# The expert stage of a 13-stage network on one NeuronCore: token rows fetched by a slot table, no rows of zeros written at the start, expert weights in 2 MB transfers

## The reference

```python
h = rms_norm(x, norm_g) * (1 + scale) + shift                 # 512 x 1024
grp = argmax(softmax(h @ w_router_group))                     # 4 groups
e_logits = (h @ w_router_expert) of the 4 experts in grp
top_p, top_i = top_k(softmax(e_logits), 2)                    # 2 of 16 experts per token
weight = p_group[grp] * top_p / sum(top_p)
y[token] = sum over its 2 experts e of weight * (silu(h @ w1[e]) * (h @ w3[e])) @ w2[e]
x = x + gate * y
```

## Time and profile before

| | us |
|---|---|
| median of three runs | 3839.18 |
| profiled execution | 3840.37 |
| its span | 3838.6 |
| first instruction of the first feed-forward | 60.5 |
| first MoE, from its first instruction to the first instruction of hgrn | 2565.0 to 2967.8 |
| its expert loop, first weight matmul | 2645.3 |
| second MoE, from its first instruction | 3431.2 |
| its expert loop, first weight matmul | 3511.8 |

### The profile page before, as it was taken

One profiled execution on the slowest core, in us unless ns is written; L12 is line 12 of the kernel. 1 busy time (PEld: TensorE's weight loads), 2 busy tenths in 40 slices (PEclk: granted clock), 3 DMA queues, 4 the chain that ended last, 5 costly groups with the idle time before them and its releaser, 6 DMA issues. The chain is left out here.

```text
span 3838.6 us, 39125 instructions
## 1 busy us (share of the span) xinstructions
PE 3356.0 (87%) x15102; PEld 2590.3 (67%) x15102; DVE 2047.6 (53%) x2698; ACT 1328.2 (35%) x1710; POOL 220.4 (6%) x241
## 2 busy tenths in 40 slices
PE   2999998899989999888999797885995987685995
PEld 2888765788878887567888585464884454544884
DVE  2555415455445544255554544545886256735886
ACT  2322215222222222243222324623884121313884
POOL 0000000000000000000000003422001000012001
PEclk9999898999999999989999897987997999886998
DMA  8333231333223323304331411025995211025995
GB/s 273 139 148 113 89 109 33 126 148 135 84 110 148 148 88 113 111 1 159 148 131 55 153 33 67 1 103 220 413 414 214 94 44 44 23 80 212 416 415 216
DMA packets 89600, 553.78 MB, mean 144 GB/s; under 512 B 9376, under 2 KB 10272, under 8 KB 41200
## 3 DMA queue, kind: packets, MB, share of 16 engines
q1 hardware_dynamic: 71760, 485.76, 32.8%
q0 software_dynamic: 13088, 49.29, 3.6%
q10 hardware_dynamic: 4608, 16.78, 1.1%
HBM read 524.49 MB, written 48.28 MB: 149 GB/s over the span
## 5 line engine op out<-in xcount | busy, mean ns | idle before, releaser
L211 PE MATMUL ffn_gate_up<-ffn_h_high,ffn_gate_up_high 128*128 128x512 f32 x1408 | 548.3, 389 | 7.1 <-DVE ffn_h_low L245 7.1
L213 PE MATMUL ffn_gate_up<-ffn_h_high,ffn_gate_up_low 128*128 128x512 f32 x1408 | 548.0, 389 | 0.0
L212 PE MATMUL ffn_gate_up<-ffn_h_low,ffn_gate_up_high 128*128 128x512 f32 x1408 | 547.8, 389 | 0.0
L2244 DVE TENSOR_TENSOR moe_low<-moe_raw,moe_high 128x2048 fp32r<-128x2048 f32 x192 | 433.7, 2286 | 38.9 <-ACT moe_high L2151 38.6
L454 ACT ACTIVATE ffn_silu_gate<-ffn_gate_up 128x512 f32<-128x512 f32 x88 | 52.7, 598 | 970.2 <-PE ffn_gate_up L213 970.2
L2151 ACT ACTIVATE moe_high<-moe_raw 128x2048 fp32r<-128x2048 f32 x192 | 364.2, 1917 | 19.4 <-PE moe_bank L213 19.4
L485 DVE TENSOR_TENSOR ffn_product<-ffn_silu_gate,ffn_gate_up 128x512 f32<-128x512 f32 x88 | 60.5, 687 | 564.4 <-ACT ffn_silu_gate L454 564.4
L211 PEld LDWEIGHTS ffn_gate_up<-ffn_h_high,ffn_gate_up_high 128*128 128x128 f32 x1408 | 264.3, 188 | 63.2 <-DVE ffn_h_low L245 8.4
L213 PEld LDWEIGHTS ffn_gate_up<-ffn_h_high,ffn_gate_up_low 128*128 128x128 f32 x1408 | 264.3, 188 | 55.1
L212 PEld LDWEIGHTS ffn_gate_up<-ffn_h_low,ffn_gate_up_high 128*128 128x128 f32 x1408 | 264.3, 188 | 55.0
L211 PE MATMUL ffn_down<-ffn_down_high,ffn_hid_high 128*128 128x512 f32 x704 | 282.7, 402 | 2.5 <-DVE x_tok L509 2.4
(11 more groups left out here) (488 smaller groups left out, 5700.9 us busy)
## 6 DMA issues: line engine op xcount, KB each, us to landing
moe_raw<-in_moe_w SPq DMA_DIRECT2D x192, 1024.0 KB, 8.0
ffn_raw_gate_up<-in_ffn_gate_up SPq DMA_DIRECT2D x88, 1024.0 KB, 6.7
ffn_ada_w<-in_ada_w SPq DMA_DIRECT2D x32, 1536.0 KB, 6.7
ffn_raw_down<-in_ffn_down SPq DMA_DIRECT2D x88, 512.0 KB, 3.3
mixer_w_raw<-in_mix_w SPq DMA_DIRECT2D x24, 1024.0 KB, 5.4
hgrn_ring<-in_hgrn_w SPq DMA_DIRECT2D x10, 2048.0 KB, 7.6
moe_xe<-moe_rows POOLq DMA_DIRECT2D x32, 512.0 KB, 9.4
moe_y<-moe_y ACTq DMA_DIRECT2D x32, 512.0 KB, 9.1
```

Source lines behind the costliest of these rows:

```text
L211: pe.matmul(out, lhsT[0], rhs[0], start=first, stop=False)
L212: pe.matmul(out, lhsT[0], rhs[1], start=False, stop=False)
L213: return pe.matmul(out, lhsT[1], rhs[0], start=False, stop=last)
L2244: dve.tensor_tensor(low[n % SPLITS][:, :, :], raw[n % RAWS][:, :, :], high[n % SPLITS][:, :, :].bitcast(FP32), ALU.subtract)\
```

## The change

At the start, POOL no longer writes zeros. `moe_rows` is gone. The 896 overflow rows of `moe_y` are zeroed by POOL in the first MoE, after the router's matmuls.

In each MoE, `h_tok` is made by transposing `hT` back on PE (32 transposes) with ACT copying it out. SP stores the 512 rows in token order in `moe_tok`, after its first three weight transfers. DVE and PE turn the routing into a table `token_in`: for each expert and slot, the token that sits there (0 where no token does). POOL then fetches each expert's 128 rows straight out of `moe_tok` with one indirect DMA. No scatter is left. The gate row's diagonal is made by eight ACT instructions. DVE does the routing in another order: what the table needs comes first, overflow and slots after it. In the combine stage DVE, not POOL, adds to x. `Own.later` and `Own.settle` issue several independent DVE instructions before waiting for them.

The weights come in 2 MB transfers, 16 KB to a partition, in a ring of three pairs (six chunks where there were seven), each pair asked for when both chunks of the pair that it replaces are split.

```diff
-            for rows in (chip.dram["moe_rows"], chip.dram["moe_y"][NE * P:SLOT_ROWS, :]):
-                pool.dma_start(rows..., chip.dram["moe_zeros"]...).then_inc(chip.rows_zeroed, 16)
...
-    RAWS, SPLITS = 7, 4
+    RAWS, SPLITS = 3, 4
+        raw_pairs = [s.sb(f"raw{i}", [P, 2, 4, 512]) for i in range(RAWS)]
+        raw = [raw_pairs[n // 2][:, n % 2, :, :] for n in range(2 * RAWS)]
...
+            for m in range(N // 2):
+                kind, e, _ = chunks[2 * m]
+                if m == RAWS:
+                    for t in range(TT):
+                        sp.wait_ge(h_tok_ready, 2 * t + 2)
+                        sp.dma_start(dram["moe_tok"][P * t:P * t + P, :], h_tok[:, t, :]).then_inc(tok_stored, 16)
+                if m >= RAWS:
+                    sp.wait_ge(w_ready, 2 * (m - RAWS) + 2)
+                sp.dma_start(raw_pairs[m % RAWS]..., dram["moe_w"][NE * layer + e, "gdu".index(kind)]).then_inc(raw_loaded[m % RAWS], 16)
...
+            for o in range(8):
+                if o >= 4:
+                    pe.wait_ge(h_tok_ready, o - 3)
+                for k in range(4):
+                    last = pe.transpose(ps[o % 4][:, k * P:(k + 1) * P], norm.hT[:, 4 * (o % 2) + k, (o // 2) * P:(o // 2 + 1) * P], chip.ident[:, :])
+                last.then_inc(h_turned, 1)
...
+            pe.wait_ge(in_slot_ready, 1)
+            for i in range(2 * TT):
+                last = pe.matmul(ps[5][:, 0:NE], in_slot[:, i, :], token_hot[:, i // TT, i % TT, :], start=(i == 0), stop=(i == 2 * TT - 1))
+            last.then_inc(token_in_done, 1)
...
 # gpsimd
-            for r, column in enumerate((mod_gain, mod[:, 0, :], mod[:, 2, :])):
-                pool.tensor_tensor(rows[r]...)                       # gain, shift, gate diagonals
-            for t in range(TT):
-                pool.tensor_tensor(h_tok[:, t, :], h_tok[:, t, :], gain_row[:, :], ALU.mult)
-                pool.tensor_tensor(h_tok[:, t, :], h_tok[:, t, :], shift_row[:, :], ALU.add)
-            for a in range(2):
-                for t in range(TT):
-                    pool.indirect_dma_start(dram["moe_rows"], ... slot_i ..., h_tok[:, t, :], None)
-            pool.wait_ge(scattered, 16 * 2 * TT)
+            if layer == 0:
+                pool.wait_ge(logits_done, 1)
+                pool.dma_start(unused, chip.dram["moe_zeros"]...).then_inc(chip.rows_zeroed, 16)
+            pool.wait_ge(tok_stored, 16 * TT)
+            pool.wait_ge(token_in_ready, 1)
             for e in range(NE):
                 if e >= 2:
                     pool.wait_ge(x_turned, e - 1)
-                pool.dma_start(xe[e % 2][:, :], dram["moe_rows"][P * e:P * e + P, :]).then_inc(xe_loaded[e % 2], 16)
+                pool.indirect_dma_start(xe[e % 2][:, :], None, dram["moe_tok"],
+                                        bass.IndirectOffsetOnAxis(token_in[:, e:e + 1], 0)).then_inc(xe_loaded[e % 2], 16)
...
 # vector, after member
+            own(dve.tensor_tensor(token_hot, hot, token_no (broadcast), ALU.mult))
+            make_low(0)
             dve.wait_ge(places_done, 1)
+            ...
+            own(dve.tensor_tensor(route, hot, place (broadcast), ALU.mult))
+            own(dve.reduce_sum(rank_of[:, :, :], route[:, :, :, :], AXX))
+            dve.tensor_tensor(in_slot, slot_no (broadcast), rank_of (broadcast), ALU.is_equal).then_inc(in_slot_ready, 1)
+            dve.wait_ge(token_in_done, 1)
+            dve.tensor_copy(token_in[:, :], ps[5][:, 0:NE]).then_inc(token_in_ready, 1)
+            make_low(1)
...
 # overflow block
+            dve.wait_ge(y_stored[1], 16 * (NE // 2))      # vector, ahead of its branch on the overflow count
+            with if_overflow(pool):                       # GpSimd now branches too
...
 # combine
-                pool.tensor_tensor(chip.x[:, t, :], chip.x[:, t, :], pair[t][:, 1, :], ALU.add)
+                dve.tensor_tensor(chip.x[:, t, :], chip.x[:, t, :], pair[t][:, 1, :], ALU.add)
```

More of the change, by code:

```diff
@@ L640, in __call__, with later, settle @@
         ins.then_inc(self.done, 1)
+        self.eng.wait_ge(self.done, self.n)
+    def later(self, ins):
+        self.n += 1
+        ins.then_inc(self.done, 1)
+    def settle(self):
         self.eng.wait_ge(self.done, self.n)
@@ L2079, in _ @@
         @block.tensor
         def _(pe):
[L2081 to L2088, removed]
-            pe.wait_ge(small_loaded, 32)
@@ L2178, in _ @@
             norm.scalar_evacuate(act, mod_gain, mod[:, 0, :])
-            for r in range(2):
-                take_row(r, 4 + 2 * r)
             make_high(0)
+            for o in range(8):
+                act.wait_ge(h_turned, o + 1)
+                act.activation(h_tok[:, o // 2, 512 * (o % 2):512 * (o % 2) + 512], ps[o % 4][:, :], ACT.Copy).then_inc(h_tok_ready, 1)
+            for k in range(KT):
+                ins = act.activation(gate_row[:, k * P:(k + 1) * P], chip.ident[:, :], ACT.Copy, scale=mod[:, 2, k:k + 1])
+            ins.then_inc(diag_ready, 1)
+            make_high(1)
             act.wait_ge(exp_in, 1)
@@ L2185, in _ @@
             act.activation(tiny[:, 1, :], tiny[:, 0, :], ACT.Exp).then_inc(exp_out, 1)
-            take_row(2, 2)
-            make_high(1)
+            act.wait_ge(row_done, 1)
+            for half in range(2):
+                act.activation(gate_row[:, 512 * half:512 * half + 512], ps[6 + half][:, :], ACT.Copy).then_inc(row_ready, 1)
             make_high(2)
@@ L2271, in _ @@
             dve.wait_ge(logits_done, 1)
-            own(dve.tensor_copy(logits[:, :, :].rearrange("p t c -> p (t c)"), ps[0][:, 0:TT * (NEG + NE)]))
+            for t in range(TT - 1):
+                own.later(dve.tensor_copy(logits[:, t, :], ps[4 + t][:, 0:NEG + NE]))
+            own(dve.tensor_copy(logits[:, TT - 1, :], ps[7][:, 0:NEG + NE]))
+            dve.sem_inc(logits_read, 1)
             dve.wait_ge(small_loaded, 32)
@@ L2275, in _ @@
             for t in range(TT):
-                own(dve.max(top[:, 0, t, :], group8[:, t, :]))
-                own(dve.max_index(top_at[:, 0, t, :], top[:, 0, t, :], group8[:, t, :]))
+                own.later(dve.max(top[:, 0, t, :], group8[:, t, :]))
+            own.settle()
+            for t in range(TT):
+                own.later(dve.max_index(top_at[:, 0, t, :], top[:, 0, t, :], group8[:, t, :]))
+            own.settle()
             own(dve.tensor_copy(top_f[:, 0, :, :], top_at[:, 0, :, 0:2]))
@@ L2380, in _ @@
                 with pe.Fori(0, NOV) as j:
+                    pe.wait_ge(over_equal, j + 1)
+                    for i in range(2 * TT):
+                        last = pe.matmul(ps[7][:, 0:1], equal[:, i, :], token_no[:, i % TT:i % TT + 1], start=(i == 0), stop=(i == 2 * TT - 1))
+                    last.then_inc(over_in_done, 1)
                     pe.wait_ge(xe_arrived, 16 * (j + 1))
@@ L2437, in _ @@
                                             bass.IndirectOffsetOnAxis(slot_i[:, a * TT + t:a * TT + t + 1], 0)).then_inc(fetched[t], 16)
-            for t in range(TT):
-                pool.wait_ge(gated, t + 1)
-                pool.tensor_tensor(chip.x[:, t, :], chip.x[:, t, :], pair[t][:, 1, :], ALU.add).then_inc(added, 1)
         @block.scalar
```

172 lines of the change are left out of this document (101 added, 71 removed).

## The result

The changed kernel took 3749.45 us (median of four runs, 3743.17 to 3757.77), before 3839.74; the ratio is 0.9766, 95% interval [0.9743, 0.9788], 90 us less. Measured once more on another chip it took 3758.3 us (3737.34 to 3765.05, five runs) against 3841.55, ratio 0.9765 [0.9739, 0.979]. The forecast was 3736, the range 3713 to 3770. The profiled execution took 3743.17 us, 97.2 less than that of before.

The account below looks back on a forecast made before the run. It took a barrier held by POOL's zeros to bound the start, a dependent chain the MoE heads, and PE, with DMA just behind, the loops. -48.5 - 54 - 1 = -103.5 us gave 3736; range 3713 to 3770.

Parts of the forecast that it names:

- rival 2: Expert loops: the ring of three is too short; 1 us wait per expert adds 32 us, 3768; chance 0.13.
- Start, -48.5: Start: barrier no longer held by POOL's zeros and loads faster, first feed-forward at 12.1 us, not 60.6.
- Heads, -27 each: Each MoE ahead of its expert loop: first weight matmul 27 us sooner, bounds -21 to -31.
- The router's end: MoE head: logits at 2586.8, not 2592.8, by 5.0 from sums of squares and 1.0 from a wait.
- the diagonals' wait: MoE head, ahead of the gate row: eight ACT diagonals at 0.26 us each, done at 2594.2.
- the places: MoE head, PE after the gate row: 16 records in 3.7 us, done at 2601.7.
- The gather: MoE head, table to first weight matmul: 9.0 us by the rows, 10 with the split, taken as 10.5.
- 4.0 from the load to PE: MoE head: 4.0 us from the load of the expert's rows at 2637.28 to PE at 2641.30.
- the 0.5 of rounding: MoE head, table to first weight matmul: 10 us for the rows' way, taken as 10.5.
- The shared port: First gather's issue beside DVE's split: 1 us delay taken; by the skill's rule 1 to 2 us worse per MoE.
- Loop, 0: Expert loops: same PE instructions and bytes, pairs asked for early enough; no change, bounds -1 and +8 us per MoE.
- Tail, -0.5 each: Loop end and combine: +3.0 for DVE's store wait, -3.6 for DVE adding alone, rounded to -0.5 us per MoE.

Follow-up runs that it names:

- After, pair held: The changed kernel with the fourth pair of weights held back until the first expert's rows have landed; 3739.32 us, ratio 0.9739.

## Why the prediction was right, and where not

The time lies in the range and 13 us above the forecast: right in sign and mostly in size, between the forecast and rival 2.

- **Start, -48.5: right** (-49.3), with its mechanism. Zeros from another queue didn't hold the barrier, zeros moved away left 11.4.
- **Heads, -27 each: mis-sized**, -18 and -19, outside the bounds of -21 to -31. Two steps failed.
  - *The router's end.* PE finished the table 46.6 us after the stage's first sum of squares, not 42.6. The router took it: it ended at 26.1 in place of 21.8. The transposes did start 5 us sooner, as forecast, but from there PE ran at half clock throughout (0.21 us a router record). The 0.16 of the earlier trace rows that I took was a mean over both levels (clock 0.69). The rest of the chain's errors nearly cancelled (transposes 1.2 more, the diagonals' wait 1.0 more, the places 1.9 less, as they happened to run at full clock).
  - *The gather.* From the table's end to the first weight matmul it took 15.7 us, not 10.7. The missed step is "4.0 from the load to PE": taken from a load with no company, while the split that I had put beside the gather also frees a pair's place. I had counted that split's time and not the 2 MB that its end sets off. "After, pair held" shows 4.6 us for it (5.4 in the second MoE). The 1 us for the split was 1.3. Another 1.2 us lay between PE's end of the table and the start of the issue, where the sum had 0.2 for the cast. Against that stood the 0.5 of rounding and another 0.5: the 4.0 was counted from the start of the load's issue and the 1.0 for the issue put on top, and the gather alone takes 4.5 and not 5.0. The rows' stores had landed 1.8 us before the table's end, not 3.
- **The shared port.** The issue's end follows the split's by 0.9 us (2555.40 and 2554.48), about an issue's own time. That fits what the Trainium skill, "SBUF — State Buffer", section "SBUF: two separate sides", says: GpSimd is kept out for the whole instruction. It cost 1.3 us, where I took 1 and gave the rule 1 to 2 more.
- **Loop, 0: wrong**, at +1.0 and +7.8, within the bounds of -1 and +8. Rival 2 had the mechanism. I set 8.5 to 10.5 us of landing against 9.8 to 11.3. The landing was 10.4, at the end of my own range, and the allowance too was taken too wide: ACT wanted the pairs g and d 8.9 and 8.8 us after they were asked for, and the step to 9.8 added time that DVE, not ACT, can wait. ACT waited for weights by 1.6 us on average (94.3 us in 60 waits of both loops). ACT's lead on PE hid most of it, and PE's idle time grew by 2.7 and 3.6 us. With 1 MB chunks the first half of a pair is asked for one split earlier and lands in 7.9 to 8.2.
- **Tail, -0.5 each: too small**, -3.4. DVE's wait for the stores cost 1.0 (last store to first gather 3.83 before, 4.83 now), not 3.0, and DVE alone was 4.4 us shorter than DVE and POOL, not 3.6.
- **Untouched stages**: -13.4 in the profiled execution, from which nothing follows for the change. The 13 other traces have 2962 to 2975. It goes with the clock: 236 us of these stages ran at half clock in the trace after, 260 to 290 in the 13 others, and the hgrn stage, for one, took 459.8 us in the two traces with 41 us of it at half clock and 462 to 465 in the twelve with 47 to 54. Among the 13 others the sum over the eight stages doesn't follow the clock (2962 us with 270, 2971 with 260), so this is not all of it. Without that luck the sum of the other terms is -84, and the two medians are -90 and -83.

What stays open: what sets how long PE waits in a loop with pairs (3.6 to 10.4 us between executions of one kernel), and what sets the time at half clock in the heads (37 to 60 us of 51 to 64 in the changed kernel and its edits). It is also not told apart whether the barrier waits for the landing of GpSimd's transfers or for something in GpSimd's queue that ends with it.

## What to carry to other kernels

When a step is moved beside another, ask what its end sets off as well as how long it takes: here a 2 MB prefetch released by a split stood in front of the one small gather that everybody waited for. In a ring whose lead is near the transfer's own time, smaller transfers asked for one at a time beat larger ones handed over in pairs, at the same bytes: the versions with 1 MB chunks are the best ones measured here, 3733 us. A saving of a few microseconds in a stage full of waits is judged in the trace, and there from one event to the next (split to gather, gather to PE) and not over the stage, since the clock moves the stage as much.

## What the runs showed of the hardware

- A barrier of all engines waited for transfers that GpSimd had issued (60.6 us), though no instruction named them, and not for those of ScalarE's queue (start at 30.3 us, when the two transfers had 28 and 41 us to go).
- ScalarE's issue of a second large transfer behind 11.5 MB held the engine for 26.5 us.
- A gather of 128 rows of 4 KB by table took 4.2 to 4.6 us from its issue to PE without company, 5.5 to 5.8 beside a split of DVE's, 7.4 to 7.7 beside the split and a 1 MB weight transfer, and 10.3 to 10.8 beside the split and 2 MB.
- A sum of squares over 128x1024 on DVE took 2.90 us beside a multiplication on GpSimd, and 1.22 without.
- Stages with the same instructions differed by up to 7 us from execution to execution (the last feed-forward took 398.3 us with 20 us at half clock, 405.3 with 33), and eight of them together by up to 19 (2954 to 2973 us).
